# An eight-layer stack changed at its two ends: order of the first loads, row factors on GpSimd, a token tile shared at the end

## What is computed

```python
def rms_norm(x, g):                     # ahead of layer 0
    return x * rsqrt(mean(x * x) + 1e-6) * g
def layer_norm(x, g, b):                # behind the last layer
    xc = x - mean(x)
    return xc * rsqrt(mean(xc * xc) + 1e-5) * g + b
```

## Time and profile before

| | us |
|---|---|
| median of 3 runs | 2441.6 |
| lowest, highest | 2439.09, 2443.31 |
| the profiled execution, its own time | 2442.03 |
| its span, first to last instruction | 2440.3 |
| mean granted clock of TensorE, share of full | 0.991 |

### The profile page before, as it was taken

One profiled execution on the slowest core, in us unless ns is written; L12 is line 12 of the kernel. 1 busy time (PEld: TensorE's weight loads), 2 busy tenths in 40 slices (PEclk: granted clock), 3 DMA queues, 4 the chain that ended last, 5 costly groups with the idle time before them and its releaser, 6 DMA issues.

```text
span 2440.3 us, 33727 instructions
## 1 busy us (share of the span) xinstructions
PE 2360.2 (97%) x13460; PEld 1915.5 (78%) x13460; DVE 963.9 (39%) x1721; ACT 900.7 (37%) x1534; POOL 947.0 (39%) x719
## 2 busy tenths in 40 slices
PE   8999999999999999999999989999999999999998
PEld 7877787868868978877787657888888888888886
DVE  5434245235634544534224773422203454422203
ACT  4334335143433553335323553322313323332311
POOL 4423344133420024433243313555554554554554
PEclk9999999999999999999999999999999999999999
DMA  5332222113210013432222212323232323323231
GB/s 147 71 68 69 80 87 86 35 37 112 91 52 2 3 36 80 103 70 44 89 87 69 70 35 74 99 93 96 86 121 87 97 93 104 100 90 103 70 137 69
DMA packets 137028, 191.84 MB, mean 79 GB/s; under 512 B 31024, under 2 KB 84656, under 8 KB 136896
## 3 DMA queue, kind: packets, MB, share of 16 engines
q1 hardware_dynamic: 127584, 183.61, 25.3%
q10 hardware_dynamic: 9312, 6.35, 1.0%
HBM read 187.84 MB, written 2.10 MB: 78 GB/s over the span
## 4 chain that ended last, share of the span: by engine, by line
issue 47%; POOL 28%; PE 22%; ACT 1%; DVE 1%; DMA 0%; POOLq 0%; SPq 0%; DVEq 0%; ACTq 0%
POOL weights_low L666 28%; PE bank L723 5%; PE bank L724 5%; PE bank L725 5%; PE bank L1431 2%; PE bank L1527 1%; PE bank L1537 1%; PE bank L1513 1%; PE bank L1541 0%; DMA weights_raw<-in_fox_w_in_dram 0%; PE bank L1447 0%; PE bank L1408 0%; PE bank L1373 0%; PE bank L927 0%; PE bank L1420 0%
## 5 line engine op out<-in xcount | busy, mean ns | idle before, releaser
L666 POOL TENSOR_TENSOR weights_low<-weights_raw,weights_high 128x512 fp32r<-128x512 f32 x688 | 926.1, 1377 | 1455.0 <-ACT weights_high L1608 1455.0
L723 PE MATMUL bank<-xt_high,weights_high 128*128 128x512 f32 (+1 forms) x1600 | 609.1, 381 | 9.6 <-POOL weights_low L666 6.9
L725 PE MATMUL bank<-xt_high,weights_low 128*128 128x512 f32 (+1 forms) x1600 | 598.7, 374 | 0.0
L724 PE MATMUL bank<-xt_low,weights_high 128*128 128x512 f32 (+1 forms) x1600 | 597.7, 374 | 0.0
L1608 ACT ACTIVATE weights_high<-weights_raw 128x1024 fp32r<-128x1024 f32 x344 | 344.8, 1051 | 681.5 <-PE bank L725 676.1
L723 PEld LDWEIGHTS bank<-xt_high,weights_high 128*128 128x128 f32 x1600 | 302.9, 189 | 74.3 <-POOL weights_low L666 13.2
L725 PEld LDWEIGHTS bank<-xt_high,weights_low 128*128 128x128 f32 x1600 | 302.4, 189 | 54.4
L724 PEld LDWEIGHTS bank<-xt_low,weights_high 128*128 128x128 f32 x1600 | 302.9, 189 | 50.1
L723 PE MATMUL bank<-weights_high,xt_high 128*128 128x512 f32 x512 | 205.4, 401 | 6.9 <-POOL weights_low L666 4.1
L725 PE MATMUL bank<-weights_high,xt_low 128*128 128x512 f32 x512 | 200.0, 391 | 0.0
L724 PE MATMUL bank<-weights_low,xt_high 128*128 128x512 f32 x512 | 199.5, 390 | 0.0
(11 more groups left out here) (391 smaller groups left out, 2962.3 us busy)
## 6 DMA issues: line engine op xcount, KB each, us to landing
weights_raw<-in_fox_w_in_dram SPq DMA_DIRECT2D x64, 512.0 KB, 5.7
weights_raw<-in_ffn_w_gate_dram SPq DMA_DIRECT2D x44, 512.0 KB, 4.0
weights_raw<-in_ffn_w_up_dram SPq DMA_DIRECT2D x44, 512.0 KB, 4.9
weights_raw<-in_ffn_w_down_dram SPq DMA_DIRECT2D x40, 512.0 KB, 4.4
weights_raw<-in_gla_w_in_dram SPq DMA_DIRECT2D x24, 512.0 KB, 4.2
weights_raw<-in_gdn_w_in_dram SPq DMA_DIRECT2D x24, 512.0 KB, 4.5
weights_raw<-in_attn_w_qkv_dram SPq DMA_DIRECT2D x24, 512.0 KB, 4.3
weights_raw<-in_conv_w_in_dram SPq DMA_DIRECT2D x24, 512.0 KB, 4.4
```

The costliest lines, as they stand in the source:

```text
L666: pool.tensor_tensor(w_lo[:, odd, k], raw[:, odd, k], w_hi[:, odd, k].bitcast(F32), ALU.subtract)\
L723: pe.matmul(out_ap, lh, rh, start=first, stop=False)
L724: pe.matmul(out_ap, lh, rl, start=False, stop=False)
L725: return pe.matmul(out_ap, ll, rh, start=False, stop=last)
```

## The change

Six things are edited. Names and lines are those above.

1. SP issues in the order: tile 0; the first 512 KB of slot 0 (with a semaphore of its own); tile 1; the rest of slot 0 as two transfers of 256 KB; slot 1; tiles 2 and 3. ScalarE's high copy of slot 0 waits for its two pieces one by one.
2. The four small loads of `load_vectors` are issued by ScalarE behind the square of tile 1, no longer at the very start.
3. In the fill, mean, epsilon and power -0.5 are made by GpSimd in two instructions of one column (`first_factor`), for tiles 0 and 1 ahead of `split(0, 0)` and for 2 and 3 ahead of `split(0, 1)`. VectorE's mean, copy, reciprocal and Newton step and ScalarE's root drop out there.
4. `keep_clock` issues 56 matmuls, not 96.
5. At the end VectorE, not GpSimd, adds the epsilon to the last tile's variance, and GpSimd only takes the power.
6. The first half of tile 2's weights and bias goes to GpSimd, the second stays with VectorE. SP stores the halves in the same order as before, the first half of tile 2 behind GpSimd's signal.

The semaphore `out_means` is replaced by the counter `pool_step`, with no other effect.

```diff
@@ -539,16 +540,28 @@
 
-            load_rows(0, 1)
+            load_rows(0)
+            def load_first_slot(parts):
+                (dst, src), (_, rest) = parts
+                sp.dma_start(raw[:, 0][dst], src).then_inc(first_weights, 16)
+                load_rows(1)
+                for m in range(2):
+                    sp.dma_start(raw[:, 0, 2 + m], rest[:, m]).then_inc(w_loaded[0], 16)
 
...
 
-                if not (isinstance(pair, int) and pair == 0):
+                at_start = isinstance(pair, int) and pair == 0
+                if at_start and not odd:
+                    load_first_slot(parts)
+                    return
+                if not at_start:
                     sp.wait_ge(w_split, 8 * pair - 4 + 4 * odd)
-                elif odd:
-                    load_rows(2, 3)
                 for dst, src in parts:
                     sp.dma_start(raw[:, odd][dst], src).then_inc(w_loaded[odd], 16)
+                if at_start:
+                    load_rows(2, 3)
 
@@ -623,9 +636,9 @@
                         sp.dma_start(rows[:, tt], x[:, tt]).then_inc(stored, 16)
-                    for n, (tt, m) in enumerate(((3, 0), (3, 1), (2, 0), (2, 1))):
+                    for done, n, tt, m in ((out_rows, 1, 3, 0), (out_rows, 2, 3, 1), (early_rows, 4, 2, 0), (out_rows, 3, 2, 1)):
                         half = slice(COLS * m, COLS * m + COLS)
-                        sp.wait_ge(out_rows, n + 1)
+                        sp.wait_ge(done, n)
                         sp.dma_start(rows[:, tt, half], x[:, tt, half]).then_inc(stored, 16)
@@ -670,17 +683,27 @@
                 pool.wait_ge(gdn["out_squares"], (24, 28, 32)[k])
-                pool.tensor_scalar(u, u, 1.0 / P, RMS_EPS, ALU.mult, ALU.add).then_inc(gdn["out_means"], 1)
-                pool.wait_ge(gdn["out_means"], k + 1)
+                pool.tensor_scalar(u, u, 1.0 / P, RMS_EPS, ALU.mult, ALU.add).then_inc(pool_step, 1)
+                pool.wait_ge(pool_step, 8 + k)
                 pool.tensor_tensor(y, u, exponents[:, OUT_BATCHES[k]], ALU.pow).then_inc(gdn["out_roots"], 1)
 
+            def first_factor(tt):
+                s = stat[:, tt:tt + 1]
+                pool.wait_ge(sumsq, tt + 1)
+                pool.tensor_scalar(s, s, 1.0 / D, RMS_EPS, ALU.mult, ALU.add).then_inc(root_in, 1)
+                pool.wait_ge(root_in, tt + 1)
+                pool.tensor_tensor(stat[:, 8 + tt:9 + tt], s, exponents[:, 0:1], ALU.pow).then_inc(root_out, 1)
+            pool.wait_ge(pool_step, 7)
             for odd in range(2):
+                for tt in (2 * odd, 2 * odd + 1):
+                    first_factor(tt)
                 split(0, odd)
...
                     split(n, odd)
-            pool.wait_ge(pool_step, 7)
             for k in range(3):
@@ -691,12 +714,15 @@
                 pool.tensor_tensor(x[:, tt], x[:, tt], norm_w[:], ALU.mult).then_inc(pool_step, 1)
-                pool.wait_ge(pool_step, 8 + tt)
+                pool.wait_ge(pool_step, 11 + tt)
                 pool.tensor_tensor(x[:, tt], x[:, tt], norm_b[:], ALU.add).then_inc(early_rows, 1)
-            pool.wait_ge(last_variance, 1)
-            pool.tensor_scalar(stat[:, 3:4], soft[:, 7:8], LN_EPS, None, ALU.add).then_inc(pool_step, 1)
-            pool.wait_ge(pool_step, 10)
+            pool.wait_ge(last_variance, 2)
             pool.tensor_tensor(stat[:, 11:12], stat[:, 3:4], exponents[:, 0:1], ALU.pow).then_inc(early_rows, 1)
+            pool.wait_ge(rows_ready, TT * (stages[-1]["filled"] // 8) + 3)
+            first = x[:, 2, 0:COLS]
+            pool.tensor_tensor(first, first, norm_w[:, 0:COLS], ALU.mult).then_inc(pool_step, 1)
+            pool.wait_ge(pool_step, 13)
+            pool.tensor_tensor(first, first, norm_b[:, 0:COLS], ALU.add).then_inc(early_rows, 1)
 
@@ -708,7 +734,7 @@
 
-            keep_clock(96)
+            keep_clock(56)
 
@@ -1603,8 +1629,11 @@
                 used = [] if isinstance(pair, int) and pair == 0 else [(w_used[odd], pair)]
-                wait_all(act, (w_loaded[odd], 32 * (pair + 1)), *used)
+                if odd or used:
+                    wait_all(act, (w_loaded[odd], 32 * (pair + 1)), *used)
                 for m in range(2):
+                    if not (odd or used):
+                        wait_all(act, (w_loaded[0], 32) if m else (first_weights, 16))
                     act.activation(w_hi[:, odd, 2 * m:2 * m + 2], raw[:, odd, 2 * m:2 * m + 2], ACT.Copy).then_inc(w_high, 1)
@@ -1775,15 +1804,13 @@
                         squares_of(0)
-                        root_of(0)
                         squares_of(1)
-                        root_of(1)
+                        load_vectors(stages[0])
                         transposed_high(0)
...
                             squares_of(tt)
-                            root_of(tt)
                         weights_high(0, 1)
@@ -1802,9 +1829,6 @@
                         transposed_high(tt)
-                if kind == "loads":
-                    if not st["full"]:
-                        load_vectors(st)
                 if kind == "project":
@@ -2322,7 +2346,7 @@
 
-                        if norm == "rms":
+                        if norm == "rms" and kind == "join":
                             dve.wait_ge(sumsq, TT * st["rms"] + tt + 1)
@@ -2347,10 +2371,11 @@
                         dve.wait_ge(root_out, st["roots"] + tt + 1)
-                        link(dve.reciprocal(y, stat[:, 12 + tt:13 + tt]))
-                        link(dve.tensor_scalar(work, y, y, -0.5, ALU.mult, ALU.mult))
-                        link(dve.tensor_scalar(work, work, stat[:, tt:tt + 1], 1.5, ALU.mult, ALU.add))
-                        link(dve.tensor_scalar(y, y, work, None, ALU.mult))
+                        if kind == "join":
+                            link(dve.reciprocal(y, stat[:, 12 + tt:13 + tt]))
+                            link(dve.tensor_scalar(work, y, y, -0.5, ALU.mult, ALU.mult))
+                            link(dve.tensor_scalar(work, work, stat[:, tt:tt + 1], 1.5, ALU.mult, ALU.add))
+                            link(dve.tensor_scalar(y, y, work, None, ALU.mult))
                         if norm == "rms":
@@ -2456,15 +2481,16 @@
                         dve.wait_ge(last_variance, 1)
+                        dve.tensor_scalar(stat[:, 3:4], soft[:, 7:8], LN_EPS, None, ALU.add).then_inc(last_variance, 1)
                         link(dve.scalar_tensor_tensor(x[:, 3], x[:, 3], soft[:, 6:7], norm_w[:], ALU.subtract, ALU.mult))
...
                         dve.wait_ge(rows_ready, TT * nth_fill + 3)
-                        link(dve.tensor_tensor(x[:, 2], x[:, 2], norm_w[:], ALU.mult))
-                        for half in row_halves:
-                            dve.tensor_tensor(x[:, 2, half], x[:, 2, half], norm_b[:, half], ALU.add).then_inc(out_rows, 1)
+                        second = row_halves[1]
+                        link(dve.tensor_tensor(x[:, 2, second], x[:, 2, second], norm_w[:, second], ALU.mult))
+                        dve.tensor_tensor(x[:, 2, second], x[:, 2, second], norm_b[:, second], ALU.add).then_inc(out_rows, 1)
                         continue
...
                     add(1)
```

More of the change, by code:

```diff
@@ L391, in six_mixer_stack @@
         w_loaded = [sem("even_slot_loaded"), sem("odd_slot_loaded")]
+        first_weights = sem("first_half_slot_loaded")
         w_high = sem("slot_high_done")
@@ L443, in six_mixer_stack @@
             "silu", "rows", "turned", "logits", "logs", "g", "sums", "columns", "exps", "factors", "spread", "qk_ready", "keys_full",
-            "keys_rows", "z_taken", "values_full", "values_rows", "selector", "out_squares", "out_means", "out_roots", "out_normed", "out_turned")}
+            "keys_rows", "z_taken", "values_full", "values_rows", "selector", "out_squares", "out_roots", "out_normed", "out_turned")}
         solve = {n: [sem(f"gdn_{n}_{q}") for q in range(4)] for n in (
```

## The result

The changed kernel took **2446.57 us** (median of 16 runs, 2444.48 to 2450.34), the kernel before, beside it on the same chip, 2442.76 (16 runs, 2438.86 to 2444.33). By the medians it is slower by 3.8 us, where +1.3 was forecast. The profiled execution took 2446.56 us, its span is 2444.8 (2440.3 before, so +4.5).

A forecast was written before the change was run, and what follows sets the result against it. TensorE, busy for 97% of the span, was taken as the bound, so only its waits at the two ends counted. Head +0.6 and tail +0.7 gave +1.3 us on the median 2441.6: 2442.9 us, range 2438.5 to 2445.5.

The forecast's parts named there:

- Part 1: At the start: the new transfer order lands tile 0 at 5.8 us, tile 1 at 8.8, tile 3 by 18.85.
- Part 2: At the start: row factors by GpSimd take 2.3 us instead of 3.64, hidden behind the first product's wait.
- Part 3: ScalarE's start: small-load issues behind tile 1's square take 2.2 us; high half starts at 13.45, against 13.88.
- late-tile rival: At the start: tile 1 lands late behind 512 KB of weights; head +2.5 instead of +0.6, 2444.8 us; chance 0.12.
- Part 4: Ahead of slot 1's split: factors 2 and 3 and the lock move its end from 27.88 to 28.45; head +0.6 us.
- Part 5: At the start: with 56 keep-clock matmuls instead of 96 TensorE stops at 8.0 us; no time on the chain.
- a sign of being wrong: First 40 us: a granted clock under 1.00 was listed as showing the prediction wrong.
- The rival's price of +5.9: From the start: clock stays at 1.2 GHz up to the end of the first half, +5.9 us, 2448.8; chance 0.06.
- Parts 6 and 7: Tail: epsilon on VectorE gains 0.2 us; tile 2's shared halves run one after the other; together +0.7 us.

The follow-up runs named there:

- e1: Changed kernel with the four small loads issued by ScalarE at the very start again; 2445.57 us.
- e2: Changed kernel with the four small loads issued behind ScalarE's high halves of slot 1; 2442.51 us.
- e5: Changed kernel with the four small loads issued by SP, behind tiles 2 and 3; 2442.49 us.
- e9: Changed kernel with the small loads reordered at the same place, three columns first, the gate's weights last; 2443.73 us.
- e10: Kernel before with only the four small loads moved, behind the second root and ahead of tile 0's copy; 2444.15 us.
- e6: e2 with the factors of tiles 2 and 3 made behind slot 1's split instead of ahead of it; 2440.94 us.
- e7: Changed kernel with small loads on SP, factors 2 and 3 behind slot 1's split, slot 1's high half ahead of squares 2 and 3; 2437.73 us.
- e3: Changed kernel with 96 keep-clock matmuls again instead of 56; 2446.63 us.
- e11: Kernel before with only the two edits of the end, epsilon on VectorE and tile 2 shared; 2443.38 us.
- e4: Changed kernel with tile 2 left to VectorE alone, the epsilon staying on VectorE; 2445.60 us.
- e8: e7 with tile 2 left to VectorE alone at the end, the epsilon staying on VectorE; 2437.87 us.

## Why the prediction was wrong

The forecast was "same", 2442.9 with a range up to 2445.5; the median lies 1.1 us above the range, and the ratio, +0.22%, just beyond the 0.2% that the prediction took for "same". Point by point:

**Part 1, transfers: right for tile 1, some 0.5 late.** Tile 0's square starts at 6.45 (said 5.8): the gain of 0.5 did not come, it was 6.35 before. Tile 1's starts at 9.31 (said 8.8). Third place did not hurt it, as the small loads were gone from its path; e1 shows that this was the condition.

**Part 2, factors: right.** 9.31 to the end of L696 at 11.38, hidden.

**Part 3, small loads: this step failed.** "I take 2.2", between 1.8 and 2.5, took both bounds from one row group, the issues at 1.23 to 3.73, when the large transfers had hardly begun (86 GB/s from 2 to 3 us); they were no bounds for the same instructions at 9 us, with SP's bulk in flight at about 400 GB/s. They took 6.1: +3.9 on the term. Two small errors stood beside it: tile 1 0.5 later, and the first issues run beside the square, not behind it (9.32 against 9.31), which gives 1.2 back, and the copy behind them 0.2. Together +3.0 on the high half (16.46 for 13.45), and +3.0 on the end of slot 1's split (31.45 for 28.45). Four runs stand behind this: e2 and e5 take the issues off that place and the loss goes; e9 shortens them by half and most of the loss goes; e10 adds them to the kernel before and adds 1.6 to the head. The text saw that "the issue sits on the chain" and then gave its length no room above. The late-tile rival had nearly the size (+2.5 on the head, measured +3.6) from another cause, a late landing of tile 1, which e1 has and the kernel after has not.

**Part 4, factors and lock: right.** From the high half to slot 1's end the sum gave 28.45 - 13.45 = 15.0; measured are 31.45 - 16.46 = 14.99 and in e9 14.96. The holds on both sides are in the trace (L694 1.29, VectorE's second product 2.29). Inside the sum one meeting went the other way round: it was the mean of tile 3 that waited for VectorE's product (1.29 for the 0.2 laid out), and the total came out all the same. What the part missed as a chance is e6 and e7: the factors need not stand there at all.

**Part 5, keep-clock: right in its effect, wrong in part of what it says.** The clock did fall below 1.00, which the prediction lists as a sign of being wrong. The 40 missing matmuls were not the reason (e3), and the fall was over before it mattered: TensorE ran behind GpSimd's quarters for a while and still came to slot 1's first one 0.46 us early (0.83 in e2, without a fall). The rival's price of +5.9 belonged to a fall up to the end of the first half, which did not come. The 56 matmuls took 5.57 us, not the 4.4 of "the same pace", and ended at 9.21, not 8.0.

**Parts 6 and 7, the tail: right in sign and mechanism.** +0.47 (e11: +0.45) for +0.7. VectorE's pair was drawn out to 3.33 by GpSimd's two halves, as said. The 0.2 that it came out better are not traced to one term. e4 parts the two: -0.3 for the epsilon, said -0.2; +0.8 for the sharing, said +0.9.

The rule of the Trainium skill's page "SBUF — State Buffer" (section "Who interferes with whom"), an exclusive lock for the whole instruction, was set against plain bandwidth sharing. The trace agrees with the lock: a column of one element per partition took 1.29 us instead of 0.19 beside VectorE's product. On the step that failed, its page "DMA: Bandwidth & Descriptors" (section "Issuing engines are not separate DMA queues") says that the time the sequencer takes to initiate a DMA is usually small beside the DMA itself. For the loads of 512 KB the trace agrees: two issues in 0.89 us (kernel before, from 0.81 on), 5.5 us and more to the landing. For the small loads no landing is recorded, but packets of ScalarE's queue moved from 13 to 19 us in the kernel after, some 9 us from the first issue to the last packet, so these transfers took longer than their issues too. What counted here was not this proportion but the stream that stood still meanwhile: up to 2.64 us in ScalarE's and 8.06 in SP's for one load of 0.5 KB or less.

**Left open.** What sets the length of an issue. With the 1024 small pieces last, it is half (e9), and the long issues end near 15 us in the kernel after, in e3 and in e5, when SP's bulk has drained (44 GB/s behind 15 us). But in e7 and e8 the one long issue of SP ended at 14.27 and 13.98, with 391 and 399 GB/s still moving. And e10 issued the same list in the same order at 11.87, with transfers still running, and took 2.5: its four issues were over at 14.40, when at most 28 of the list's 1344 packets had moved (the others moved behind 15 us), so an issue need not wait until the pieces ahead of it are gone. e2 and e6, with the same list at nearly the same moment (18.5, 17.9), took 3.8 and 2.3. That the filling of the queues decides is argued, not shown. Nor was it tried to split the gate's weights from the columns in different streams.

## What to carry to other kernels

An instruction that issues a DMA has a length, and the stream that holds it stands still for that long: price it from an issue under the same load, not from the first microseconds, and put small loads into a stream with slack (here SP, behind its own bulk) and long lists of tiny pieces last. Where two engines hand over in a chain, order the work of each by what the last in the chain needs: of the 5.1 us that e7's start gains on the kernel before, 2.7 come from letting GpSimd run its eight quarters without a break, and 2.3 from starting them earlier. Don't give half a tile to GpSimd to relieve VectorE when both read two operands from SBUF: the halves go one after the other.

## What was not expected of the hardware

- The issue of one load of 0.5 KB took from 0.33 us (e9, at 9.38) to 2.58 (e3, at 10.82) and 8.06 (e5, SP, at 6.86).
- With small pieces in flight at the start, a tile in third place landed at 12.99 (e1), without them at 9.31, at the same issue time (1.75 us).
- The grant of the lower clock level came and went within ten microseconds at the start (0.69 and 0.63 of full in e3, 1.00 from 25 us on) without any cost in time. A fall between 25 and 29 us, on the products with slot 1's last quarters, cost 0.5 us (e5, e9).
- A profile drifts by up to 2.5 us against another in code that is identical, where the clock's short dips lie differently. A difference of a microsecond has to be read at landmarks.
